# First two tiles of an encoder trunk in another order, with slabs kept for the second tile

## What is computed

```python
def mixer_ab(x, ...):
    hcomb = einsum('bsd,de->bse', x, w_in)           # 1536 columns
    u, v = gelu(hcomb[..., :512]), gelu(hcomb[..., 512:1024])
    z = hcomb[..., 1024:]
    a = chunk_spatial_gate(u, v, g_v, w_s, b_s)      # u * (w_s @ norm(v) + b_s), per head
    b = multiscale_pool(z, w_pool, pool_scale)
    return einsum('bse,ed->bsd', concatenate([a, b]), w_out)

def mixer_c(x, w_in, conv_w, w_out):
    gate_b, gate_c, hv = split(einsum('bsd,de->bse', x, w_in), 3)
    conv = conv3(gate_c * hv, conv_w)
    return einsum('bse,ed->bsd', gate_b * conv, w_out)

def swiglu(x, w_gate, w_up, w_down):
    return einsum('bsf,fd->bsd', silu(x @ w_gate) * (x @ w_up), w_down)

for layer in range(2):
    x = x + rmsnorm(mixer(rmsnorm(x, g[0])), g[1])
    x = x + rmsnorm(swiglu(rmsnorm(x, g[2])), g[3])
```

## Time and profile before

| | us |
|---|---|
| median of three runs | 4064.33 (4059.5 to 4079.43) |
| the profiled execution | 4059.64 |
| its span, slowest core | 4058.0 |
| spans of the eight cores | 4044.7 to 4058.0 |
| TensorE busy | 3926.5 |
| VectorE busy / ScalarE busy | 1857.9 / 1733.5 |

### The profile page before, as it was taken

The page is one execution under the profiler, slowest core; times in us unless marked ns, Lnnn a source line. Parts: engine busy times, 40 slices in busy tenths (PEclk is TensorE's granted clock), DMA queues, the critical chain, the costliest instruction groups (busy, mean ns, idle before and its releaser), DMA issues.

```text
span 4058.0 us, 58466 instructions; the slowest of 8 cores (4044.7 to 4058.0 us)
## 1 busy us (share of the span) xinstructions
PE 3926.5 (97%) x19879; PEld 1941.1 (48%) x19879; DVE 1857.9 (46%) x3228; ACT 1733.5 (43%) x2846; POOL 245.8 (6%) x542
## 2 busy tenths in 40 slices
PE   7878999999999999999999999999999999999998
PEld 3333444444444444444444445544445655456655
DVE  5622662372463455345336237336336354363432
ACT  6412552362453454445335336435335444353432
POOL 0000220010010000001001002001001000010000
PEclk9899999999999999999999999999999999999999
DMA  8898688654454454455455446555446666456665
GB/s 271 253 221 232 178 221 205 172 191 153 151 188 154 144 178 163 158 168 175 151 171 170 154 143 217 182 172 177 151 161 199 202 206 206 155 189 202 202 210 190
DMA packets 187394, 748.93 MB, mean 185 GB/s; under 512 B 22720, under 2 KB 29888, under 8 KB 182080
## 3 DMA queue, kind: packets, MB, share of 16 engines
q1 hardware_dynamic: 185504, 719.49, 54.1%
q0 software_dynamic: 1600, 25.69, 4.4%
HBM read 723.08 MB, written 73.40 MB: 196 GB/s over the span
## 4 chain that ended last, share of the span: by engine, by line
PE 90%; DMA 5%; DVE 1%; issue 1%; ACT 1%; SPq 0%; DVEq 0%; POOL 0%; ACTq 0%; POOLq 0%
PE PS L493 90%; DMA XR<-wsrc 4%; DMA RG<-wbf 1%; SPq L535 0%; ACT VN L506 0%; DVE RG L531 0%; DMA X<-wsrc 0%; DVE XG L522 0%; DVE ARENA L511 0%; DVE TT L511 0%; DVE H L511 0%; DVE X L511 0%; ACT L526 0%; ACT GB L504 0%; ACT L506 0%
## 5 line engine op out<-in xcount | busy, mean ns | idle before, releaser
L493 PE MATMUL PS<-XG,RG 128*128 128x512 bf16 (+4 forms) x12800 | 2555.7, 360 | 63.8 <-DMA RG<-wbf 26.6
L493 PEld LDWEIGHTS PS<-XG,RG 128*128 128x128 bf16 x12800 | 1254.5, 98 | 1325.5 <-issue 102.2
L493 PE MATMUL PS<-ARENA,RG 128*128 128x512 bf16 (+2 forms) x4816 | 980.9, 362 | 2.4 <-DVE ARENA L511 2.4
L493 PEld LDWEIGHTS PS<-ARENA,RG 128*128 128x128 bf16 x4816 | 471.5, 98 | 489.9 <-issue 4.7
L506 ACT ACTIVATE SQO<-PS 128x512 bf16<-128x512 f32 (+2 forms) x416 | 233.6, 565 | 822.2 <-PE PS L493 816.3
L511 DVE TENSOR_TENSOR SQO<-SQO 128x512 bf16<-128x512 bf16 (+2 forms) x351 | 142.2, 405 | 879.7 <-ACT SQO L506 866.7
L506 ACT ACTIVATE H<-PS,CST 128x512 f32<-128x512 f32 (+2 forms) x416 | 270.4, 652 | 9.3 <-PE PS L493 7.4
L511 DVE TENSOR_TENSOR H<-H,R 128x1024 f32<-128x1024 f32 (+2 forms) x208 | 231.3, 1139 | 84.3 <-ACT R L527 84.3
L506 ACT ACTIVATE TT<-PS 128x512 f32<-128x512 f32 (+2 forms) x190 | 107.4, 566 | 354.1 <-PE PS L493 353.2
L511 DVE TENSOR_TENSOR ARENA<-PS,TT 128x512 bf16<-128x512 f32 (+2 forms) x183 | 118.7, 649 | 279.7 <-PE PS L493 252.1
L511 DVE TENSOR_TENSOR ARENA<-PS,GB 128x512 bf16<-128x512 f32 (+2 forms) x183 | 118.4, 647 | 275.5 <-PE PS L493 236.4
(11 more groups left out here) (80 smaller groups left out, 1961.5 us busy)
## 6 DMA issues: line engine op xcount, KB each, us to landing
RG<-wbf SPq DMA_DIRECT2D x711, 512.0 KB, 3.5
RG<-wbf SPq DMA_DIRECT2D x200, 704.0 KB, 4.5
RG<-wbf SPq DMA_DIRECT2D x104, 768.0 KB, 5.2
y<-X SPq DMA_DIRECT2D x36, 512.0 KB, 8.4
XR<-xin SPq DMA_DIRECT2D x64, 264.0 KB, 5.9
wbf<-RG SPq DMA_DIRECT2D x32, 512.0 KB, 9.7
XR<-wsrc SPq DMA_DIRECT2D x15, 1024.0 KB, 13.0
CB<-wsrc SPq DMA_DIRECT2D x13, 1024.0 KB, 12.4
```

Source lines behind the costliest of these rows:

```text
L493: return lambda e: e.matmul(out, lhsT, rhs, start=start, stop=stop)
```

## The change

- V and Z slabs are acquired once and used by tiles 0 and 1 (`two_slabs`, `slabs=`). `zvu` is split; the new order is V(0), norm of tile 1, `vnorm(0)`, Z(0), U(0), V(1), Z(1), `mix(0)`, `vnorm(1)`, `out0(0)`, `chain0(0)`, U(1), `mix(1)`, `out0(1)`, `chain0(1)`. Results of the second tile get places of their own (`CV`, `GT`, parts of `X[0]`); half of `vnorm` of these tiles goes to VectorE.
- Seven feed-forward slabs (`LEAD`), five in the ring and two in `R` and `VN`, serve chunks 0 to 6 of tile 0 and then of tile 1; chunks 7 to 21 are paired. `down0(0)` follows in one piece; its slabs 4 to 7 are kept for `down0(1)`, which takes 7, 6, 5, 4, 0, 1, 2, 3.
- A slab's write-back is emitted at the next `acquire` and waits for the main matmul emitted last. Staging sets differ.
- A background cast comes after 22 us of matmuls until the last down slab has been written back, then after 8.
- Tile 2 is normalised into `CB[1]` and `X[2]` (`xgn`), and its V, Z, U come between chunks 3 and 4 of `cin(0)`.
- The scheduler's cost table has one DMA pipe for both queues, at other rates.

```diff
-CAST_PACE = 10.0
+CAST_PACE = 8.0
...
-        GB = [sb(f"GB{r}", [128, 512], F32) for r in range(2)]
-        CV = [sb(f"CV{r}", [128, 512], F32) for r in range(2)]
-        TT = [sb(f"TT{r}", [128, 512], F32) for r in range(2)]
+        GTA = sb("GT", [128, 2048], F32)
+        GB = [GTA[:, 512 * r:512 * r + 512] for r in range(2)]
+        TT = [GTA[:, 1024 + 512 * r:1536 + 512 * r] for r in range(2)]
+        CVA = sb("CV", [128, 1024], F32)
...
         STG = [flat2(X[2][:, 4:8, :]), flat2(CB[1]).bitcast(F32), flat2(CB[0]).bitcast(F32),
-               flat2(XR[:, 0:4, :]), flat2(XR[:, 4:8, :])]
-        bSTG = [bX[2][4:8], bCB[1], bCB[0], bXR[0:4], bXR[4:8]]
-        stage_set = lambda j: (0, 1, 2) if j < FF0 else (2, 3, 4)
+               flat2(XR[:, 0:4, :]), flat2(XR[:, 4:8, :]), flat2(X[2][:, 0:3, :])]
+        bSTG = [bX[2][4:8], bCB[1], bCB[0], bXR[0:4], bXR[4:8], bX[2][0:3]]
+        def stage_set(j):
+            if j >= CC0:
+                return (0, 5)
+            if j < FF0:
+                return (0, 1, 2)
+            return (0, 2) if j < FF0 + 3 else (0, 2, 3, 4) if j < FF0 + 9 else (2, 3, 4)
         bYS = bufs(8)
...
-            if not cast_todo or cast_clock[0] < CAST_PACE:
+            if not cast_todo or cast_clock[0] < (CAST_PACE if bWBF[DN0 + 7].w else 22.0):
...
-        def acquire(j):
+        wb_todo = []
+
+        def write_back():
+            while wb_todo:
+                j, dst, ap, pages = wb_todo.pop(0)
+                k = rnext("wb", 4)
+                after = Buf()
+                after.w = P.main_pe
+                dma("sp", dst, ap, f"wb{k}", 256 * SLAB_COLS[j], reads=pages + [after], writes=[bWBF[j], bWBS[k]], cls=0)
+
+        def acquire(j, home=None):
+            write_back()
             u = SLAB_COLS[j]
             n = u // 256
-            if ring_pos[0] + n > NRP:
-                ring_pos[0] = 0
-            p0 = ring_pos[0]
...
                     h = halves[rnext("stage", 12) % len(halves)]
                     dma("sp", STG[h][:, 0:w], flat_ap(wsrc)[:, i * w:(i + 1) * w], f"st{h}", 512 * w,
                         writes=bSTG[h] + [bSTS[h]], cls=0)
-                    copy("dve", ap[:, i * w:(i + 1) * w], STG[h][:, 0:w], w // 2, bSTG[h], pages, cls=0)
+                    if j >= CC0 and i == 1:
+                        act(ap[:, i * w:(i + 1) * w], STG[h][:, 0:w], AF.Copy, w, bSTG[h], pages, cls=0)
+                    else:
+                        copy("dve", ap[:, i * w:(i + 1) * w], STG[h][:, 0:w], w // 2, bSTG[h], pages, cls=0)
                 if O0 <= j < FF0:
                     fold(ap.rearrange("p (k c) -> p k c", k=8), pages)
-                k = rnext("wb", 4)
-                dma("sp", flat_ap(wbf), ap, f"wb{k}", 256 * u, reads=pages, writes=[bWBF[j], bWBS[k]], cls=0)
+                wb_todo.append((j, flat_ap(wbf), ap, pages))
             else:
                 assert bWBF[j].w is not None, (j, cast_todo, cast_clock)
...
+        def xgn(t):
+            if t == 2:
+                cb = flat2(CB[1])
+                return [cb[:, 528 * c:528 * c + 528] for c in range(7)] + [X[2][:, 3, :].bitcast(BF16)], \
+                       [bCB[1][528 * c // 512:(528 * c + 527) // 512 + 1] for c in range(7)] + [[bX[2][3]]]
+            return [XG[t % 2][:, c, :] for c in range(8)], [[b] for b in bXG[t % 2]]
+
         def n1_apply(t, src=None, bsrc=None):
             W = tile_width(t)
-            xg, bxg = XG[t % 2], bXG[t % 2]
+            xg, bxg = xgn(t)
             src, bsrc = (XR, [[b] for b in bXR]) if src is None else (src, bsrc)
             for c in range(8):
-                stt(xg[:, c, 0:W], src[:, c, 0:W], G(0, c), RS1[:, 0:W], ALU.mult, ALU.mult, W,
-                    bsrc[c] + [bCST] + bRS1, [bxg[c]])
+                stt(xg[c][:, 0:W], src[:, c, 0:W], G(0, c), RS1[:, 0:W], ALU.mult, ALU.mult, W,
...
         def zvu(t, after_v=None):
+            zvu_v(t, after_v)
+            vnorm(t)
+            zvu_z(t)
+            zvu_u(t)
+
+        def two_slabs(j):
+            return [acquire(j + s) for s in range(2)]
+
+        def zvu_v(t, after_v=None, slabs=None):
             T = TILE_T[t]
             halo = t == HALO_TILE
-            TW = T + 32 if halo else T + 16
-            xg, bxg = XG[t % 2], bXG[t % 2]
-            ic, bic = ICE[t % 2], bICE[t % 2]
+            xg, bxg = xgn(t)
             nj = T // 128
-            v3, vpages = [], []
-            for s in range(2):
-                slab, pages = acquire(VC0 + s)
-                v3.append(slab.rearrange("p (k c) -> p k c", k=4))
-                vpages.append(pages)
+            slabs = slabs or two_slabs(VC0)
+            v3 = [slab.rearrange("p (k c) -> p k c", k=4) for slab, _ in slabs]
+            vpages = [pages for _, pages in slabs]
             offs = [8 + 128 * jc for jc in range(nj)] + ([T + 32] if halo else [])
             nv = len(offs)
-            for jc, o in enumerate(offs):
-                b = next_bank()
-                fns = [mmop(PS[:, b, 0:512], xg[:, kc, o:o + 128], v3[kc // 4][:, kc % 4, :], kc == 0, kc == 7)
-                       for kc in range(8)]
...
+        def vnorm(t):
+            nv = TILE_T[t] // 128 + int(t == HALO_TILE)
+            for h in range(4):
+                for jc in range(nv):
                     k = jc * 4 + h
                     v = Vt[:, jc, h * 128:(h + 1) * 128]
-                    act(VN[:, jc, h * 128:(h + 1) * 128], v, AF.Identity, 128, bV[jc] + [bRV, bNM], [bVN[jc]],
+                    if h % 2 and t < 2:
+                        ts(VN[:, jc, h * 128:(h + 1) * 128], v, RV[:, k:k + 1], ALU.mult, 128, bV[jc] + [bRV, bNM],
+                           [bVN[jc][h]], s2=NM[:, k:k + 1], op1=ALU.add)
+                        continue
+                    act(VN[:, jc, h * 128:(h + 1) * 128], v, AF.Identity, 128, bV[jc] + [bRV, bNM], [bVN[jc][h]],
                         scale=RV[:, k:k + 1], bias=NM[:, k:k + 1])
...
+        def out_stage(T, slab0, nk, per_slab, rhs_fn, rhs_bufs, gpost, home={}, have={}, order=range(8)):
+            got = {}
+            for q, i in enumerate(order):
+                j = i // per_slab
+                if j not in got:
+                    got[j] = have.get(j) or acquire(slab0 + j, home.get(j))
+                slab, pages = got[j]
+                st = slab.rearrange("p (k c) -> p k c", k=nk)
                 b = next_bank()
                 lhs_group(b, T, st, (i % per_slab) * 128, rhs_fn, rhs_bufs, pages, nk)
...
             Te = TILE_T[t] + int(t == HALO_TILE)
             x = t % 3
-            out_stage(Te, DN0, NFF, 1, lambda kc: hc[kc][:, 0:Te], lambda kc: bhc[kc], 3, rng)
-            if rng[-1] == 7:
-                xs = lambda c, n: X[x][:, c:c + n, 0:Te]
-                chain(Te, 4, xs, [[b] for b in bX[x]], xs, bX[x], XG[t % 2], bXG[t % 2])
+            got = out_stage(Te, DN0, NFF, 1, lambda kc: hc[kc][:, 0:Te], lambda kc: bhc[kc], 3, have=have, order=order)
+            xs = lambda c, n: X[x][:, c:c + n, 0:Te]
+            chain(Te, 4, xs, [[b] for b in bX[x]], xs, bX[x], XG[t % 2], bXG[t % 2])
+            return got
...
-        n1_first()
-        zvu(0, load_wsp)
+        home = lambda ap, bb, c: (flat2(ap[:, c:c + 2, :]).bitcast(BF16), bb[c:c + 2])
+        n1_first(0)
+        v01 = two_slabs(VC0)
+        zvu_v(0, load_wsp, v01)
         load_x(1, 0, XR1, bXR1)
-        n1(1, XR1, bXR1)
-        mix(0)
-        out0(0)
-        chain0(0)
-        zvu(1)
-        mix(1)
-        for f in range(2):
-            ffn0_chunk(0, f)
-        out0(1)
-        chain0(1, XR1, bXR1)
-        for f in range(2, 11):
-            ffn0_chunk(0, f)
+        n1_first(1, XR1, bXR1)
+        vnorm(0)
+        z01 = two_slabs(ZC0)
+        zvu_z(0, z01)
+        zvu_u(0, home(X[0], bX[0], 4))
+        rt1 = CVA[:, :].bitcast(BF16).rearrange("p (g w) -> p g w", g=4)
+        brt1 = [bCV[0], bCV[0], bCV[1], bCV[1]]
+        ab0 = flat2(X[0][:, 6:8, :]).bitcast(BF16).rearrange("p (g w) -> p g w", g=4)
+        ab0 = [ab0[:, g, :] for g in range(4)]
+        bab0 = [[bX[0][6 + g // 2]] for g in range(4)]
+        zvu_v(1, None, v01)
+        zvu_z(1, z01, rt1, brt1)
+        mix(0, ab0, bab0)
+        vnorm(1)
+        out0(0, {0: home(H, bH, 4), 1: home(H, bH, 6)}, ab=ab0, bab=bab0)
+        chain0(0, cls=0)
+        u1 = GTA[:, :].rearrange("p (g w) -> p g w", g=4)
+        zvu_u(1, None, u1, bGB + bTT)
+        mix(1, u=u1, bu=bGB + bTT, f2=RS1, bf2=bRS1)
+        out0(1, {}, rt1, brt1)
+        chain0(1, XR1, bXR1, cls=0)
+        LEAD = 7
+        spare = {0: (flat2(Rt), bR), 1: (flat2(VN), flat(bVN))}
+        first = [ffn0_chunk(0, f, acquire(FF0 + f, spare.get(f))) for f in range(LEAD)]
+        for f in range(LEAD):
+            ffn0_chunk(1, f, first[f])
         cast_todo.extend(range(NDIRECT, NSLAB))
-        for f in range(11, NFF):
+        for f in range(LEAD, NFF):
             ffn0_chunk(1, f, ffn0_chunk(0, f))
-        for f in range(11):
```

(15 more changed lines are left out.)

181 lines of the change are left out of this document (101 added, 80 removed).

## The result

The changed kernel is faster: the ratio of its runs to those of the kernel before is 0.9927, 95% interval 0.9899 to 0.9954. The profiled run took 4035.0 us against 4059.6, so 25 us were gained where 66 were forecast, and the time lies above the range (3964 to 4032 us). Rows are of core 3 unless another is named; the strips of before are of core 7, its slowest.

The account below looks back on a forecast made before the run. The prediction took the start as the loss: waits for `VN`, then data with DMA nearly full, then `XG`. Gains of 61 and 9 less 4 for casts made 66 us: 4059.6 to 3994 us, range 3964 to 4032.

Parts of the forecast that it names:

- the 33 us of DMA time saved by kept slabs: Start: 15 re-reads of chunk, V, Z and down slabs vanish, 33 us of DMA, so chunk pairs just keep up.
- the price of the moved casts: After the start: about seven casts come later, DMA share reaching 0.91 in 600 to 735 us; 4 us charged, 0 to 12.
- First stage: 22.7 to 144.3 us: waits for `VN` of the second tile go; end at 120 instead of 137.4, gain 17 us.
- I give nothing for the other waits: First stage: no gain counted for waits on slab casts and VectorE's residual work, VectorE being busy 84.9 of 121.7 us.
- the rival: First stage: VectorE or ScalarE replaces data as the limit, gain 5 instead of 17, `chain0(1)` uncovered; 4012 us, chance 0.18.
- Chunks: Feed-forward of tiles 0 and 1: 44 chunks in 151.8 us plus statistics and 2 us of waiting, ending at 275.5 us.
- I charge nothing: Chunks and down projection: write-backs waiting for matmuls cost nothing beyond the 52 us, with 10 us as bound.
- First down projection: Down projection of tile 0: slab loads, write-backs and casts make it 52 us for 38 us of matmuls, ending at 327.
- DMA share near 1: Sign of being right: chunks of both tiles done near 276 us with the DMA engines almost fully used.
- Third tile: From 474.1 us: waits for `XG` and the half clock after them vanish, gain 9 us.
- the 17 us that the prediction set as its sign: Sign of being wrong: re-reads landing later than 17 us between 330 and 640 us, with idle behind them.
- The rival on this rule: After the start: postponed casts saturate the DMA near a share of 0.98, losing 78 us; 4068 us, chance 0.05.

Follow-up runs that it names:

- a_cls1: Changed kernel with the post-norm chains of the first two tiles at ordinary instead of raised priority; ratio to the kernel before 0.9960.
- a_vn_act: Changed kernel with all of `VN` of the first two tiles normalised on ScalarE again instead of half on VectorE; median span 4038.8 us, no ratio.
- a_reread7: Changed kernel, but tile 1 reads its first seven chunk slabs again instead of using the kept ones; ratio to the kernel before 0.9941.
- b_pace: Kernel before with only the new rule for background casts (22 us of matmuls apart, later 8); 4050.4 us in the one run that counts.
- a_rule10: Changed kernel with the old rule for background casts (one after each 10 us of matmuls throughout); ratio to the kernel before 0.9961.
- b_third: Kernel before with only the third tile's part (`xgn`, and V, Z, U of tile 2 between chunks 3 and 4 of `cin(0)`); 4051.3 us profiled.
- a_gap35: Changed kernel with background casts 35 us of matmuls apart instead of 22 until the last down slab is written back; ratio to the kernel before 0.9961.
- all three: Changed kernel with write-backs at once, kept down slabs in order 4, 5, 6, 7 and start casts 35 us apart; ratio to the kernel before 0.9900.

## Why the prediction was wrong

Two steps failed most: the 33 us of DMA time saved by kept slabs, which with the new order gave 1 to 6 us behind the first stage, and the price of the moved casts, 4 us against 18.5 measured.

- **First stage: right mechanism, mis-sized.** 17 us forecast (137 to 120), 11 measured (136 to 125). The waits for `VN` went. "I give nothing for the other waits" was the step: `chain0(0)` at priority makes the squares late (2.5 and 2.9 us, ended by ScalarE), and `a_cls1` without it reaches 120. VectorE was busy 81.2 of 103.8 us, and with less of its work in `a_vn_act` the stage got longer. So of the rival only the priority of `chain0` is borne out.
- **Chunks: 275.5 forecast, 291.3 measured** on the slowest core. 6.5 of the 16 us are the first stage, 6.2 the wait at 222 us behind a write-back. "I charge nothing" for the write-back's wait for TensorE failed; it cost 2 to 8 us up to `down0(0)`, within its bound of 10.
- **First down projection: about right.** 52 us forecast, 57.4 measured (291.3 to 348.7), with 16 us of waits where "some 10" were to be seen.
- **The time it was held against was too early.** The 388.3 us of before count three chunks behind 377.93. Four stood there, and the first began late and slow:

```profile
377.93 5.22 PE L493 MATMUL PS<-XG,RG 128*128 128x512 bf16 x16 [3.44 <-DMA RG<-wbf]
...
383.20 10.52 PE L493 MATMUL PS<-XG,RG 128*128 128x512 bf16 x48
```

All was done at 393.6 us. With that, the end forecast for `down0(0)`, 327 us, would have been a gain of 67 and not 61, and the forecast still 5 us lower; on the slowest cores 393.6 - 348.7 = 45 were gained. The error hides 5 us of the miss.
- **Kept slabs: the mechanism fell.** 33 us of DMA time were taken out of the sum at 3.14 us per MB. But DMA time counts only where TensorE waits for it, and from 155 to 167 us the engines stood idle, since a ring full of kept slabs lets nothing in. `a_reread7` puts seven of them back and `down0(0)` ends 2 us later; the others (V, Z, four more chunk slabs, four down slabs) have no run of their own, and all of them with the new order gave 1 to 6 us between the first two marks. The mark "DMA share near 1" until 276 us was plainly wrong, 0.74 where it had been 1.00, and a wrong sign too: `b_pace` has 0.98 and gets through the chunks as fast. What lowered the share is the new order (0.85 in `a_rule10`), and then the casts. The casts are what shortened this stage: 2.9 MB of them fewer up to 375 us (8.39 before, 5.51 below), at 8.6 us per MB, are 25 us, and `b_pace` gained 32.
- **Kept down slabs 7, 6, 5, 4: not seen.** The forecast ends at `down0(0)` and takes over the rest as it was. The order costs 5 us.
- **Third tile: right.** 9 forecast, 8.9 in `b_third`, and no wait for `XG` at the third tile is left.
- **The moved casts: the step that failed most after the start.** 4 us forecast, from 0 to 12; 18.5 measured, 15 of them gone in `a_rule10`. The share reckoned for 600 to 735 us, 0.91, came out exactly. What failed is what was read from it: near 0.98 alone would re-reads be late. The windows show what the average hides: the share is 0.93 in one part and 0.95 in another, and there TensorE waits (the last row is the stretch of the average):

```profile
483.00:536.00 53.00, 48.72 (x228) 21.83 (x226) 36.94 (x57) 27.55 (x44) 13.55 (x31) 0.97 0.93 222
...
570.00:640.00 70.00, 70.00 (x326) 31.71 (x325) 16.55 (x25) 16.23 (x25) 3.89 (x8) 1.00 0.87 208
640.00:735.00 95.00, 86.79 (x401) 38.49 (x399) 35.30 (x61) 39.88 (x57) 3.94 (x8) 1.00 0.95 209
600.00:735.00 135.00, 126.79 (x586) 56.62 (x585) 40.57 (x69) 46.99 (x69) 5.89 (x12) 1.00 0.91 209
```

Re-reads of 512 KB landed later in 640 to 735 us, after 14.3 us in the median; on the same core before it was 8.0 (the second line). That is still below the 17 us that the prediction set as its sign.

```profile
RG<-wbf SPq DMA_DIRECT2D x22, 512.0 KB, 14.3
RG<-wbf SPq DMA_DIRECT2D x19, 512.0 KB, 8.0
```

Each DMA engine serves the software and the hardware queue in turn, says the Trainium skill ("DMA: Bandwidth & Descriptors", "SWDGE vs HWDGE vs iDMA"). The traces agree in effect: the casts landed later there too, after 12.7 us against 9.9, which fits two queues that share the engines, neither ahead of the other; no run tests the rule by itself. The rival on this rule had the right mechanism and too high a price (78 us), as it took the state of the start as its measure. The page "HBM Reference" of the Trainium skill, section "Specifications (TRN2)", gives some 358 GB/s to each core of a busy pair. SyncE's queue moved 49.55 MB in 62.5% of 245 us, 3.09 us per MB or 324 GB/s, near the 3.14 used; but slices of 6 us of the same view moved up to 415 GB/s, so these traces don't settle the page's figure.

The measured parts, by the marks: 45 gained up to `down0(0)`, 9 for the third tile, 11 lost between them (the order's 5 and the casts' 4 among it), 18.5 lost in the iteration. That is 24.5, and the spans' medians differ by 24.2. After `mix(3)` nothing is left: four iterations of 322.8 became 322.4, but the one from `mix(9)` to `mix(10)` went from 312.4 to 317 us in every kernel with the changed code, and in neither `b_` kernel; 3.4 us of it are a new wait for `GT` behind ScalarE. Why was not tried.

What stays open: the 12 us of `a_cls1` behind its first stage, and why casts 35 us apart cost time between `down0(0)` and `mix(2)` (9 us in `a_gap35`, 3 and 9 with the write-back at once); so the write-backs' wait for TensorE doesn't explain it, and no run isolates the cause.

## What to carry to other kernels

Background work that is postponed is a debt: price it where it lands, by the share in the busiest 50 to 100 us there and not by the average, before counting the gain where it left. DMA time that is saved counts only where the compute engine waits for it, and the share doesn't tell that: ask whether something can be issued there, since a buffer filled with data to be kept is itself what stops the loads. And when three edits each give nothing, try them together: a wait removed alone was handed to the next of them here, and all three gave 12 us at `mix(2)`, 8 of the median span.

## What the runs showed of the hardware

- A write-back of 0.5 MB took 19.45 us from issue to landing in the chain, at DMA shares of 0.6 to 0.9, while the median one landed after 8.0 us; the median is no bound for what a buffer waits for.
- The engine time that a cast costs isn't constant. Before, in 130 to 375 us, it was 8.6 us per MB at a share of 0.97. In `a_rule10`, at 0.84 to 0.87, it was 8.1 to 8.3 (cores 1, 3 and 7). In the changed kernel the same rows give 14.4% of 245 us for 5.51 MB, 6.4 us per MB at 0.77, so the share alone doesn't set it. SyncE's queue took 3.1 to 3.2 us per MB in all of them:

```profile
q1 hardware_dynamic: 10495, 49.55, 62.5%
q0 software_dynamic: 336, 5.51, 14.4%
```
